# One scan over every second state on VectorE, with its inputs and its even outputs formed on TensorE

## What is computed

```
u  = xin                                   # (256 positions, 64 groups, 16 channels)
ab = exp(lambda * dt)                      # complex, one per group and state: 64 groups x 64 states
bb = (ab - 1) / lambda * b                 # complex input matrix, 64 x 16 per group
s[t] = ab * s[t-1] + bb @ u[t]             # complex, diagonal: the scan over 256 positions
y[t] = Re(c @ s[t]) + d * u[t]             # 16 channels per group
out  = gelu(y) * sigmoid(gelu(y) @ w_glu + b_glu)
```

## Time and profile before

| | |
|---|---|
| median of 3 runs | 3102.59 us (3102.37 to 3105.28) |
| the profiled execution, its own time | 3104.03 us |
| its span in the trace | 3102.3 us |
| TensorE busy | 2969.5 us (96%) |
| VectorE busy | 1890.8 us (61%) |
| ScalarE busy | 1370.2 us (44%) |
| GpSimd busy | 362.7 us (12%) |
| mean granted TensorE clock | 0.982 of full speed |

### The profile page before, as it was taken

How to read it: one execution, slowest core, us unless ns; L and a number is a source line. 1 busy time by engine, 2 the same in 40 slices (tenths; PEclk the granted TensorE clock), 3 DMA queues, 4 the chain that set the end, 5 groups by cost and what they waited for, 6 DMA issues and landing times.

```text
span 3102.3 us, 33328 instructions
## 1 busy us (share of the span) xinstructions
PE 2969.5 (96%) x13300; PEld 2422.5 (78%) x13300; DVE 1890.8 (61%) x2064; ACT 1370.2 (44%) x1573; POOL 362.7 (12%) x390
## 2 busy tenths in 40 slices
PE   8778878999999999999999999999999999999998
PEld 7565656887887888888888878788887888888886
DVE  6699798444665455555545667877565545455455
ACT  6432323446444444444444544444445544444443
POOL 0595793001100000000000000001000000000000
PEclk9888899999999999999999999999999999999999
DMA  9334335655555555555555755666655556555554
GB/s 301 91 119 130 111 122 160 192 184 157 188 197 183 195 182 194 189 185 187 186 181 189 232 171 170 196 192 207 204 176 184 190 183 194 185 196 183 190 189 150
DMA packets 290458, 559.92 MB, mean 180 GB/s; under 512 B 17664, under 2 KB 24576, under 8 KB 289664
## 3 DMA queue, kind: packets, MB, share of 16 engines
q1 hardware_dynamic: 290304, 557.80, 55.8%
HBM read 555.63 MB, written 2.10 MB: 180 GB/s over the span
## 4 chain that ended last, share of the span: by engine, by line
PE 76%; issue 10%; DVE 7%; POOL 6%; ACT 1%; DMA 1%; SPq 0%; DVEq 0%; POOLq 0%; ACTq 0%
PE ACC L601 73%; DVE WL L1205 2%; PE TB L557 2%; POOL TMP L453 1%; POOL TMP L454 1%; POOL SS L458 1%; POOL SS L456 1%; DVE SS L456 1%; DVE TMP L453 1%; DVE TMP L454 1%; DVE SS L458 1%; DVE CA L1574 0%; PE TB L625 0%; DMA RAW<-in_w_in_dram 0%; ACT WH L810 0%
## 5 line engine op out<-in xcount | busy, mean ns | idle before, releaser
L1205 DVE TENSOR_TENSOR WL<-RAW,WH 128x1024 fp32r<-128x1024 f32 (+1 forms) x1024 | 1274.7, 1261 | 866.6 <-ACT WH L810 864.8
L810 ACT ACTIVATE WH<-RAW 128x1024 fp32r<-128x1024 f32 (+1 forms) x1024 | 1062.3, 1053 | 1024.3 <-PE ACC L601 885.4
L601 PE MATMUL ACC<-WH,XTH 128*128 128x512 f32 (+1 forms) x2720 | 1087.2, 400 | 89.2 <-DVE WL L1205 83.3
L601 PE MATMUL ACC<-WL,XTH 128*128 128x512 f32 (+1 forms) x2720 | 1069.8, 393 | 0.0
L601 PE MATMUL ACC<-WH,XTL 128*128 128x512 f32 (+1 forms) x2720 | 1069.7, 393 | 0.0
L601 PEld LDWEIGHTS ACC<-WH,XTH 128*128 128x128 f32 x2720 | 519.0, 191 | 219.0 <-DVE WL L1205 77.8
L601 PEld LDWEIGHTS ACC<-WH,XTL 128*128 128x128 f32 x2720 | 519.3, 191 | 110.9
L601 PEld LDWEIGHTS ACC<-WL,XTH 128*128 128x128 f32 x2720 | 519.7, 191 | 102.8
L601 PE MATMUL ACC<-WH,YAH 128*128 128x512 f32 x864 | 343.5, 398 | 19.0 <-DVE WL L1205 18.9
L601 PE MATMUL ACC<-WL,YAH 128*128 128x512 f32 x864 | 339.5, 393 | 0.0
L601 PE MATMUL ACC<-WH,YAL 128*128 128x512 f32 x864 | 339.5, 393 | 0.0
(11 more groups left out here) (222 smaller groups left out, 1554.0 us busy)
## 6 DMA issues: line engine op xcount, KB each, us to landing
RAW<-in_w_in_dram SPq DMA_DIRECT2D x256, 512.0 KB, 4.3
RAW<-in_w_mlp_in_dram SPq DMA_DIRECT2D x128, 512.0 KB, 4.1
RAW<-in_w_mlp_out_dram SPq DMA_DIRECT2D x128, 512.0 KB, 4.4
RAW<-in_w_up_dram SPq DMA_DIRECT2D x128, 512.0 KB, 4.1
RAW<-in_w_down_dram SPq DMA_DIRECT2D x128, 512.0 KB, 4.3
RAW<-in_w_gate_dram SPq DMA_DIRECT2D x96, 512.0 KB, 4.4
RAW<-in_w_branch_dram SPq DMA_DIRECT2D x48, 512.0 KB, 3.8
RAW<-in_w_out_dram SPq DMA_DIRECT2D x32, 512.0 KB, 4.5
```

The source lines that it names most:

```text
L601: ins = e.matmul(ACC[:, 2 * (b % 2) + half, 0:n], p[:, k, xs], q[:, t, 0:n], start=(k == 0 and m == 0), stop=(k == nk - 1 and m == 2))
L810: e.activation(WH[u % NSPL][:, :, 0:n], RAW[u % NRAW][:, :, 0:n], ACT.Copy).then_inc(hi, 1)
L1205: e.tensor_tensor(l, r, h, ALU.subtract).then_inc(lo, 1)
```

## The change

The recurrence is taken over two positions at a time. With positions 2m and 2m + 1 written as even and odd, only the odd states are scanned, with the square of `ab` as factor:

- s[2m+1] = ab² s[2m-1] + (bb u[2m+1] + ab bb u[2m])
- y[2m] = Re(c ab s[2m-1]) + Re(c bb) u[2m], and y[2m+1] = Re(c s[2m+1])

So 128 states a tile are scanned, all 32 tiles in the same instructions, on VectorE alone; GpSimd has no scan. The 128 odd positions are 16 chunks of 8 places, and the chunk is innermost in memory: the 16 elements of one place lie side by side (64 bytes), the next tile 512 bytes on. There are 7 steps of 1024 elements, 15 of 64 and 7 of 960, four instructions each (116 in all). A new table of `b` by states (`BS`, two transfers of 512 KB) serves for `ab` times `b` (VectorE, six instructions of 1024 elements), which TensorE transposes into `ABT`, and for the factor `K0` of the even outputs. GpSimd and VectorE also form `ab` times `c` (`CA_`). `PR` now shares its place with the gate biases `GB`, and the high and low parts `YAH`, `YAL` share theirs with `BS` and `ABT`.

```
     early.append((CST[:, :], a["cst"], ld["cst"]))
+    early += [(BS[:, k, :], a["s5_bs"][:, k, :], ld["s5bt"]) for k in range(2)]
+    early += [(CT[:, k, :], a["s5_ct"][:, k, :], ld["s5c"]) for k in range(2)]
     early += [(X[:, 0, 512 * k:512 * k + 512], a["s5_bt"][:, 512 * k:512 * k + 512], ld["s5b"]) for k in range(4)]
...
-    early += [(CT[:, k, :], a["s5_ct"][:, k, :], ld["s5c"]) for k in range(2)]
...
-    at("s5_mat", 14, 5)
-    at("s5_mat", 23)
+    at("s5_mat", 14, 9)
+    at("ab", 23, 2)
+    at("s5_mat", 24)
     at("ut", 25)
-    for use in range(4):
-        start, pace = 27 + (use // 2) * (47, 45)[use % 2], (0.85, 0.9)[use % 2]
-        at(("bu", use), start, 4, pace)
-        at(("scan", use), start + 5, 35, pace)
-        at(("y", use), start + 6 + int(35 / pace))
+    for r in range(4):
+        at(("bu", r), 27 + r)
+    at("k0", 33)
+    at("scan", 31, 71, 0.76)
+    for n in range(4):
+        at(("y", n), 31 + int(71 / 0.76) + n // 2)
...
@@ TensorE: inputs of the scan (32 products a task, four tasks) @@
+            for qq in range(2):
+                q = 2 * r + qq
+                for ri in range(2):
+                    for k in range(2):
+                        for i in range(4):
+                            rows, cs = slice(32 * i, 32 * i + 32), slice((2 * qq + ri) * P, (2 * qq + ri) * P + P)
+                            ins = e.matmul(to[i][0][:, cs], (ABT, BT)[k][rows, ri, q, :], UP[rows, q, k * P:k * P + P],
+                                           start=(k == 0), stop=(k == 1))
...
@@ TensorE: outputs (56 products for each of four n) @@
+                for j, rows in tiles:
+                    e.matmul(t[rows, out(0, P)], K0[rows, q, :], ue[rows], start=True, stop=False)
+                for ri in range(2):
+                    for j, rows in tiles:
+                        e.matmul(t[rows, out(16, P)], CA_[:, ri, 32 * j:32 * j + 32], SS[:, ri, j, 0:112], start=False, stop=False)
+                for ri in range(2):
+                    for j, rows in tiles:
+                        e.matmul(t[rows, out(1, 16)], CA_[:, ri, 32 * j:32 * j + 32], SS[:, ri, j, 112:127], start=False, stop=(ri == 1))
+                for ri in range(2):
+                    for j, rows in tiles:
+                        ins = e.matmul(t[rows, out(P, 2 * P)], CT[:, ri, 32 * j:32 * j + 32], SS[:, ri, j, :],
+                                       start=(ri == 0), stop=(ri == 1))
...
@@ ScalarE: ab (4 copies of 512), ut (4 copies of 512, and 8 more of 256 that reorder) @@
+            for k in range(4):
+                t = TB[TBU["ut", k][0]]
+                for m in range(2):
+                    ins = e.activation(UP[:, 2 * k + m, :].rearrange("p (k i c) -> p k i c", k=2, i=8),
+                                       t[:, m * L:m * L + L].rearrange("p (c i k) -> p k i c", i=8, k=2), ACT.Copy)
...
@@ ScalarE: s5_bu, before the first copy into SS @@
+            if r == 0:
+                e.wait_ge(ca_done, 2)
...
@@ VectorE: the scan @@
+            Sv = SS[:, :, :, :].rearrange("p a j (i c) -> p a j i c", c=16)
...
+            def step(dst, src, power, w, pause):
+                rr = AP[:, 0, :, power].unsqueeze(1).unsqueeze(3).to_broadcast([P, 2, 32, w])
+                ii = AP[:, 1:3, :, power].unsqueeze(3).to_broadcast([P, 2, 32, w])
...
+                e.tensor_tensor(t0, src, rr, ALU.mult)
...
+                e.tensor_tensor(t1, src[:, ::-1], ii, ALU.mult).then_inc(scan, 1)
...
+                e.tensor_tensor(dst, dst, t0, ALU.add).then_inc(scan, 1)
...
+                e.tensor_tensor(dst, dst, t1, ALU.add).then_inc(scan, 1)
...
+            for i in range(1, 8):
+                yield from step(Sv[:, :, :, i, :], Sv[:, :, :, i - 1, :], 0, 16, True)
+            for c in range(1, 16):
+                yield from step(Sv[:, :, :, 7, c:c + 1], Sv[:, :, :, 7, c - 1:c], 7, 1, False)
+            for i in range(7):
+                yield from step(Sv[:, :, :, i, 1:16], Sv[:, :, :, 7, 0:15], i, 15, True)
...
@@ VectorE, s5_mat: six of 1024 elements (one, two, two, one to a step), then behind c and ab * c @@
+            e.wait_ge(ck, 4)
+            e.tensor_tensor(CTV[0], CZ[0], CZ[1], ALU.subtract).then_inc(c_done, 1)
+            yield
+            e.scalar_tensor_tensor(out=CTV[1], in0=CZ[2], scalar=-1.0, in1=CZ[3], op0=ALU.mult, op1=ALU.subtract).then_inc(c_done, 1)
+            yield
+            e.wait_ge(ak, 4)
+            e.tensor_tensor(CAV[0], CZ[0], CZ[1], ALU.add).then_inc(ca_done, 1)
+            e.tensor_tensor(CAV[1], CZ[3], CZ[2], ALU.subtract).then_inc(ca_done, 1)
...
@@ GpSimd, s5_mat: the four products for c as before, then @@
+            e.wait_ge(c_done, 2)
+            e.tensor_tensor(CZ[0], CTV[0], wr, ALU.mult).then_inc(ak, 1)
+            e.tensor_tensor(CZ[1], CTV[1], wi, ALU.mult).then_inc(ak, 1)
+            e.tensor_tensor(CZ[2], CTV[0], wi, ALU.mult).then_inc(ak, 1)
+            e.tensor_tensor(CZ[3], CTV[1], wr, ALU.mult).then_inc(ak, 1)
...
@@ VectorE: outputs, 16 of 128 elements in place of 8 of 256 @@
+                    u = UT[:, q, :].rearrange("p (c i k) -> p k c i", i=8, k=2)[:, k]
+                    y = t[:, m * L + k * P:m * L + k * P + P].rearrange("p (i c) -> p c i", i=8)
```

More of the change, by code:

```diff
@@ L612, in ut @@
             yield
[L614 to L623, removed]
-                for ri in range(2):
[L625 to L628, removed]
@@ L630, in s5_y, with ab @@
-        def s5_y(use):
-            lane, base = use % 2, 8 * use
-            e.wait_ge(scan[lane], (use // 2 + 1) * SCAN)
-            e.wait_ge(c_done, 2)
-            t, done = bank(("y", use), 0)
-            for m in range(2):
[L636 to L640, removed]
+        def ab():
+            e.wait_ge(ab_done, 2)
+            e.wait_ge(ld["cst"], 16)
+            for k in range(4):
+                t, done = bank("ab", k)
+                for m in range(4):
+                    q = 4 * (k % 2) + m
+                    ins = e.transpose(t[:, m * P:m * P + P], ABZ[2 * (k // 2)][:, q * P:q * P + P], IDENT)
+                ins.then_inc(done, 1)
+                if k % 2:
+                    yield
@@ new lines, in s5_y, with out @@
+        def s5_y(n):
+            if n == 0:
+                e.wait_ge(scan, SCAN)
+                e.wait_ge(ca_done, 2)
+                emptied(e, "k0", 0)
+            t, done = bank(("y", n), 0)
+            for m in range(2):
+                q = 2 * n + m
+                ue = UT[:, q, :].rearrange("p (c i k) -> p k i c", i=8, k=2)[:, 0]
+                tiles = [(4 * q + i, slice(32 * i, 32 * i + 32)) for i in range(4)]
+                def out(lo_, hi_):
+                    return slice(m * L + lo_, m * L + hi_)
+                for j, rows in tiles:
[9 more added lines that the diff above has]
+                        ins = e.matmul(t[rows, out(P, 2 * P)], CT[:, ri, 32 * j:32 * j + 32], SS[:, ri, j, :],
+                                       start=(ri == 0), stop=(ri == 1))
@@ L783, in _ @@
                  "pm": pool_means, "wg": pool_groups}
-        for use in range(4):
-            tasks["bu", use] = lambda use=use: s5_bu(use)
-            tasks["y", use] = lambda use=use: s5_y(use)
+        for n in range(4):
+            tasks["bu", n] = lambda n=n: s5_bu(n)
+            tasks["y", n] = lambda n=n: s5_y(n)
         for hg in range(2):
@@ L896, in u_out, with ab @@
                 yield
+        def ab():
+            for k in range(4):
+                t = filled(e, "ab", k)
+                freed(e.activation(ABT[:, k // 2, 4 * (k % 2):4 * (k % 2) + 4, :], t[:, :].rearrange("p (q s) -> p q s", q=4), ACT.Copy),
+                      "ab", k)
+                if k % 2:
+                    yield
         def ut():
@@ L930, in s5_gelu @@
         def s5_gelu():
-            for use in (2, 3):
-                emptied(e, ("y", use), 0)
+            for n in range(4):
+                emptied(e, ("y", n), 0)
             e.activation(UT[:, :, :], UT[:, :, :], ACT.Gelu_apprx_tanh).then_inc(ug_done, 1)
@@ L1654, in _ @@
                  "wg": pool_groups, "place_c": lambda: place("yc2", GBT, 6), "place_a": lambda: place("ya2", CA, 6)}
-        for use in range(4):
-            tasks["y", use] = lambda use=use: s5_y(use)
-        for use in (0, 2):
-            tasks["scan", use] = lambda use=use: s5_scan(use)
+        for n in range(4):
+            tasks["y", n] = lambda n=n: s5_y(n)
         for hg in range(2):
```

255 lines of the change are left out of this document (143 added, 112 removed).

## The result

The changed kernel takes 2963.81 us (median of 4 runs, 2963.04 to 2965.3), the one before 3102.48 us in the same session. The ratio is 0.9552, with a 95% interval of 0.9535 to 0.9568: 138.7 us less. The forecast was 2964.

The account below looks back on a forecast made before the run. It took TensorE's waits for VectorE and low clock to bound 87 to 529 us: 261.2 + 36.3 + 5 = 302.5 us in place of 441.2, 138.7 less, giving 2964 us as a median; range 2944 to 2998.

Parts of the forecast that it names:

- scan inputs: TensorE in the scan stretch: 128 products of half the columns, 10 us in place of 16.8, bounds 8.4 and 16.8.
- outputs: TensorE in the scan stretch: 224 products in place of 128, 13.8 us, bounds 7 and 28.
- `k0`: TensorE products for the factor of the even outputs: 64 x 0.062 = 3.9 us, bounds 2 and 8.
- spatial mixer: Its TensorE products in the scan stretch: 4 x (1.11 + 1.05) = 8.6 us, the same as before.
- waits and gaps between pieces: TensorE's waits left in the scan stretch, at the spatial mixer and gate evictions: 5 us kept.
- the front: Units 14 to 31: moved `c` table and new VectorE products cost nothing, covered by units of lead and time until unit 27.
- Wide instructions at the packed rate: VectorE's scan: 28 instructions of 1024 elements at 1.16 us and 28 of 960 at 1.09, 63 us.
- The clock came back: Rival, 8%: in the scan stretch TensorE's clock stays at 0.90, products take 331 us in place of 297.5: 2997 us.
- Strided rates: Rival, 7%: VectorE's wide scan instructions take 2.4 us per 1024 elements, 38 us of waits plus clock loss: 3020 us.
- VectorE as the bound: Rival, 2%: units 31 to 67 and 88 to 123, wide instructions take 3.8 us, kernel gets slower: 3139 us.
- the transfers: Rival, 1%: something else, such as transfers at 191 GB/s and a share of 0.61, fills the scan stretch: no change.
- The rule on PSUM patterns: Skill rule cited for the front: non-contiguous PSUM patterns slow matmuls; by it the upper bounds would be the ones to take.

Follow-up runs that it names:

- GpSimd beside: Changed kernel with unused GpSimd work added beside the scan, three sums of 256 elements behind each of 88 units: 3000.2 us, ratio 0.9671.
- the runs with more products: Changed kernel with each product of the 14 wide scan steps issued twice, three or four times: 2966.1, 2991.9 and 3027.2 us.

## Why the prediction was right, point by point

**The bound and the way it went: right.** The waits for VectorE were what the stretch lost, and with the scan at 83 us of VectorE (forecast 81) they went. Behind 118 us TensorE is at full clock and its waits are below 1 us.

**The sum: right as a sum, by errors that cancel.** It was 302.5 us from unit 26's forecast start, without units 122 to 125. Measured: 398.35 - 86.7 - 4 x 2.72 = 300.8 us. Term by term:

| term | forecast | measured |
|---|---|---|
| 96 units | 261.2 | 261.2 (0.2267 us apart) |
| front late: unit 26, wait before unit 27 | 0 | 6.0 + 2.4 |
| scan inputs | 10 | 8.0 (4 x 2.0) |
| outputs | 13.8 | 13.1 (6.52 + 6.56) |
| `k0` | 3.9 | 1.2 |
| spatial mixer | 8.6 | 4.7 |
| waits and gaps between pieces | 5 | 4.2 (what is left) |

The 6.0 us include 1.6 us of the transposes of `ab`, which were to be covered by idle time ahead of unit 26. The terms named for the prediction's own range do not add up to 2946 and 2984 but to some 2951 (13.4 us below the forecast) and 2986 (21.8 above it); nothing hangs on that here.

**The step that failed: the front.** The prediction put the six new VectorE products and the moved table at nothing and named two covers: units of lead on VectorE, and time until unit 27. It priced VectorE's work by its own durations. Missing was that GpSimd's products now fell beside VectorE's instructions, each of which then took up to 2.3 us. The earlier trace rows had shown it: L1337 took 2.09 us where L1338 takes 1.21, and GpSimd's L1703 (82.22 to 83.31) lay beside it. GpSimd's products for `c` were done at 65.7, as forecast, but VectorE was to have `c` ready at 73 us and had it at 84.1, `ab` times `c` at 84 and was at 96.9. The mark set for the front, unit 31 by 115 us, was missed (117.8) without making the forecast wrong, since the other terms were too dear. The mark "`y` at 125 near 390 us" held for its start, 391.8; the outputs end at 398.3, where the prediction's sum puts 400.

**Products counted wrongly.** An fp32 product of this kind stands in the trace as two records. The prediction held its 224 products of the outputs against 128 records of before, at 0.062 us a record. After, they are 448 records in 13.1 us, 0.029 us each: twice as many as it had, and half as long. For the scan inputs it halved the columns; in sum they are the same as before (4 x 32 x 128 = 8 x 8 x 256). The 8.0 us lie just under its lower bound of 8.4, for another reason than fewer columns (last section). Both terms were near by luck, and `k0` was not near.

**The spatial mixer: mis-sized by reading.** 1.05 and 1.11 us are durations; the next product starts 0.81 us after the eight (151.45 - 150.64). Distances were used for the weights, and should have been here. The same error is in the 33.3 us of before, so the loss to be regained there was nearer 150 than 146.7 us.

**Wide instructions at the packed rate: right** (1.22 us, forecast 1.16 as a distance, measured 1.14), small ones 0.28 against 0.3. The layout alone was worth 47 us in the kernel before. What the other parts were worth was only tried by putting their cost back: GpSimd beside cost 36 us, a number of wide instructions as for all 256 positions 28 us. These do not add up to the gain and need not, since cover lies between them.

**The rivals.** The clock came back to 1.00. Its case was not empty, though: with one row group at a time it was 0.74 in the stretch concerned. Strided rates and VectorE as the bound did not occur, and the transfers did not fill the stretch: they ran at 196 GB/s and a share of 0.66 while TensorE hardly waited; the runs with more products show that some 32 us more on VectorE would have been free, and 64 us not. The rule on PSUM patterns speaks of matmuls. What the runs show is reads of PSUM by the other engines, by form and in order of time:

```profile
94.26 2.34 ACT L923 ACTIVATE X<-TB 128x256 f32<-128x256 f32 x8
...
L1442 DVE SCALAR_TENSOR_TENSOR UT<-UT,VEC,TB 128x128 f32<-128x128 f32 x16 | 4.5, 343 | 14.6 <-PE TB L649 14.6
...
L1463 DVE SCALAR_TENSOR_TENSOR GR<-TB,VEC,GR 128x128 f32<-128x128 f32 x8 | 2.2, 341 | 0.0
```

ScalarE's eight reordering copies of 256 elements went by at 0.29 us each, the lower bound. VectorE's outputs of 128 elements took 0.343 us with a 64-byte distance in PSUM against 0.341 for L1463 without. So the upper bounds were not needed here.

## What to carry to other kernels

Work given to GpSimd is not free for VectorE: price each GpSimd instruction that reads SBUF by what it costs VectorE, and compare with VectorE doing it itself (1.14 against 1.5 us here). Put what is scanned side by side in memory and take fewer, wider instructions, and count the slack of the engine that feeds the bound one before moving anything onto it; here some 32 us in 250 were free and 64 were not. When a transfer is moved forward, look at what the work that waits for it will then run beside.

## What the runs showed of the hardware that was not expected

- Before, the scan inputs of one unit were 8 products of 256 columns, which touched two of the four row groups, and took 2.1 us. After, they are 32 products of 128 columns over all four groups, twice the columns, and take 2.0 us. That the row groups are the whole cause was not tried; pairs of one group gave 2.3 us, eight in a row 6.9 at a clock of 0.91.
- TensorE's clock fell to its lower level in a stretch in which the engine counted as busy for 96% of the time (62.5 of 65 us), with products of one row group at a time and no wait ahead of it. In the other rows shown here it is low behind waits.
- A VectorE instruction of 64 elements took 1.9 us beside a GpSimd product of 1024 and 0.22 us without it.
